# Seven block products in place of eight for three pairs of FFN chunks

## What is computed

```python
def swiglu(h, w_in, w_out):
    a, b = jnp.split(h @ w_in, 2, axis=-1)
    return (jax.nn.silu(a) * b) @ w_out
...
x = x + 0.5 * swiglu(rms_norm(x, norm_g[l, 0]), ffn_w_in[l, 0], ffn_w_out[l, 0])
```

## Time and profile before

| | us |
|---|---|
| median of 3 runs | 1055.21 (1054.1 to 1055.28) |
| the profiled execution, its own time | 1053.35 |
| its span | 1051.4 |
| PE busy in it | 1040.1 |
| DVE busy | 598.2 |
| ACT busy | 525.5 |
| POOL busy | 73.4 |

### The profile page before, as it was taken

How to read it: one execution, slowest core, us unless ns; L and a number is a source line. 1 busy time by engine, 2 the same in 40 slices (tenths; PEclk the granted TensorE clock), 3 DMA queues, 4 the chain that set the end, 5 groups by cost and what they waited for, 6 DMA issues and landing times.

```text
span 1051.4 us, 14153 instructions
## 1 busy us (share of the span) xinstructions
PE 1040.1 (99%) x5156; PEld 865.4 (82%) x5156; DVE 598.2 (57%) x833; ACT 525.5 (50%) x692; POOL 73.4 (7%) x108
## 2 busy tenths in 40 slices
PE   9999999999999999999999999999999999999997
PEld 7888888888888888888888888888888888888886
DVE  5554454677576564455467765544566656445544
ACT  7434434657475554434456554344356655443443
POOL 0041000000013000000000291000000000000000
PEclk9999999999899999999999999999999999999999
DMA  7686757457401366555545665555446146655541
GB/s 243 239 214 208 218 187 249 145 175 225 136 2 41 120 202 198 191 168 199 183 150 188 221 204 193 184 198 190 170 160 200 42 140 201 199 183 177 199 160 41
DMA packets 128709, 182.45 MB, mean 174 GB/s; under 512 B 5960, under 2 KB 100272, under 8 KB 128544
## 3 DMA queue, kind: packets, MB, share of 16 engines
q1 hardware_dynamic: 127040, 176.18, 50.5%
q0 software_dynamic: 1456, 5.72, 2.4%
q10 hardware_dynamic: 176, 0.05, 0.0%
HBM read 180.34 MB, written 1.59 MB: 173 GB/s over the span
## 4 chain that ended last, share of the span: by engine, by line
PE 97%; DVE 2%; ACT 1%; issue 0%; POOL 0%; POOLq 0%; DVEq 0%; ACTq 0%
PE inb L403 16%; PE inb L405 16%; PE inb L404 16%; PE acc L403 13%; PE acc L405 13%; PE acc L404 13%; PE acc L613 2%; PE tb L512 2%; PE tb L625 2%; PE inb L640 2%; PE inb L637 1%; PE tb L592 1%; PE tb L397 1%; PE acc L397 0%; DVE tlo L1346 0%; PE inb L824 0%
## 5 line engine op out<-in xcount | busy, mean ns | idle before, releaser
L1329 DVE TENSOR_TENSOR wlo<-raw,whi 128x2048 fp32r<-128x2048 f32 x108 | 250.0, 2315 | 233.6 <-ACT whi L935 233.6
L935 ACT CAST whi<-raw 128x2048 fp32r<-128x2048 f32 x108 | 206.5, 1912 | 217.5 <-PE acc L405 117.8
L403 PE MATMUL inb<-whi,thi 128*128 128x512 f32 x720 | 281.7, 391 | 0.0
L405 PE MATMUL inb<-whi,tlo 128*128 128x512 f32 x720 | 280.5, 390 | 0.0
L404 PE MATMUL inb<-wlo,thi 128*128 128x512 f32 x720 | 280.2, 389 | 0.0
L405 PEld LDWEIGHTS inb<-whi,tlo 128*128 128x128 f32 x720 | 135.1, 188 | 28.4
L404 PEld LDWEIGHTS inb<-wlo,thi 128*128 128x128 f32 x720 | 135.2, 188 | 28.0
L403 PEld LDWEIGHTS inb<-whi,thi 128*128 128x128 f32 x720 | 135.2, 188 | 28.0
L1312 DVE TENSOR_TENSOR wlo<-raw,whi 128x2048 fp32r<-128x2048 f32 x55 | 129.1, 2352 | 43.8 <-ACT whi L922 43.5
L403 PE MATMUL acc<-whi,ghi 128*128 128x512 f32 x320 | 128.5, 402 | 0.0
L405 PE MATMUL acc<-whi,glo 128*128 128x512 f32 x320 | 125.1, 391 | 0.0
(11 more groups left out here) (231 smaller groups left out, 980.1 us busy)
## 6 DMA issues: line engine op xcount, KB each, us to landing
raw<-in_ffn_w_in SPq DMA_DIRECT2D x174, 512.0 KB, 4.7
raw<-in_ffn_w_out SPq DMA_DIRECT2D x88, 512.0 KB, 4.0
raw<-in_nsa_w_in SPq DMA_DIRECT2D x20, 512.0 KB, 4.1
raw<-in_fox_w_kvf SPq DMA_DIRECT2D x16, 512.0 KB, 4.3
raw<-in_nsa_cmp_w SPq DMA_DIRECT2D x8, 512.0 KB, 4.8
raw<-in_nsa_w_out SPq DMA_DIRECT2D x8, 512.0 KB, 4.5
raw<-in_fox_w_q SPq DMA_DIRECT2D x8, 512.0 KB, 4.5
raw<-in_fox_w_out SPq DMA_DIRECT2D x8, 512.0 KB, 4.6
```

The costliest lines, as they stand in the source:

```text
L403: pe.matmul(o, lh, rh, start=start, stop=False, skip_group_check=True)
L405: return pe.matmul(o, ll, rh, start=False, stop=stop, skip_group_check=True)
L935: act.copy(whi[u % RING][:, :], raw[u % RING][:, :]).then_inc(s_hi, 1)
L1329: dve.tensor_tensor(wlo[u % RING][:, :], raw[u % RING][:, :], whi[u % RING][:, :].bitcast(F32), ALU.subtract).then_inc(s_lo, 1)
```

## The change

In each FFN three pairs of chunks (2 and 3, 5 and 6, 8 and 9) are projected together. Seen as blocks, a pair is a product of tokens (2 tiles x 2 halves of the 1024 columns, A11 to A22) and weights (2 halves of 512 rows x 512 gate or 512 up columns, B11 to B22). Seven products M1 to M7 replace eight. M1, M2 and M3 take B11, B21 and B22 as loaded; M5, M7, M6 and M4 take the combinations T1 to T4, which DVE makes (`t1_weights` to `t4_weights`); the token sides are A11, A12, A22 and the sums S1 to S4, which POOL makes once per FFN from the tokens, joined again from `thi` and `tlo` and scaled by rstd (`token_sums`). PE turns rstd into a row for that (`rstd_rows`). The results are put together on ACT and DVE: M1 to `u3`, M5 to `c22`, then `c12`, `u3` and `c22`, and C21 (`u3` again).

An ordinary chunk stands between two pairs. The loops are written out for all five engines. Ordinary units use two `raw` buffers; the third holds T1 and then T4. B11 and B12 go to `nat`, B21 to `xn`, B22 to the first part of `work`, loaded by SP with two DMAs of 512 KB each. T3 and T2 overwrite B12 and B11. The hidden halves get a buffer of four column blocks (`fhi`, `flo`). In FFN 2 the tables of the forget gate wait until the token sums are split. The last chunk is an ordinary one.

In the lists below, `wlo<-nat` or `wlo<-work` is the lo part of a weight unit, `flo<-tb` that of a turned hidden tile, `blo` that of a token sum; `raw<-nat`, `nat<-work,nat` and `nat<-nat` are T1, T3 and T2, and `raw<-xn,nat` is T4.

The core of the diff:

```diff
+KINDS = "nnsnsnsn"
...
+def ffn_order():
+    order = []
+    for kind, j, rows in SEGMENTS:
+        if kind == "n":
+            order += [("a", j), ("b", j)] + [("o", r) for r in rows]
+        else:
+            order += [("M1", j), ("M5", j), ("o", rows[0]), ("M2", j), ("M6", j)]
+            order += [("o", r) for r in rows[1:]] + [("M3", j), ("M7", j), ("M4", j)]
+    return order + [("o", r) for r in LAST_ROWS]
...
+            def product(f, j, name, a, bank, start, stop):
+                u = U_FFN[f] + UNIT_OF[name, j]
+                a_hi, a_lo = token_block(a)
+                pe.wait_ge(s_lo, u + 1)
+                for k in range(4):
+                    col = slice(k * CW, (k + 1) * CW)
+                    mm = three(bank[:, :], a_hi[:, k], a_lo[:, k], whi[u % RING][:, col], wlo[u % RING][:, col],
+                               start and k == 0, stop and k == 3)
+                mm.then_inc(s_used, 1)
...
+            def pair_turn(f, j, t):
+                pe.wait_ge(s_g, 2 * (NSEG * f + STAGES[j]) + t + 1)
+                pe.wait_ge(s_glo, NTURNS * f + turns_before(j) + t)
+                for k in range(4):
+                    mm = pe.transpose(tb[0][:, k * P:(k + 1) * P], (c22 if t else c12)[:, k * P:(k + 1) * P],
+                                      ident[:, :])
+                mm.then_inc(s_gt, 1)
+            def ffn_chunk(f, j, rows):
+                b, i = U_FFN[f], STAGES[j]
+                kind, before, _ = SEGMENTS[i - 1]
+                pairs = len(PAIRS) * f + sum(p < j for p in PAIRS)
+                u = b + UNIT_OF["a", j]
+                pe.wait_ge(s_lo, u + 1)
+                if kind == "s":
+                    pe.wait_ge(s_u3, pairs)
+                rows4(u % RING, 0, 0, inb[0][:, :])
+                if kind == "s":
+                    pe.wait_ge(s_c21, pairs)
+                rows4(u % RING, 0, 1, inb[1][:, :]).then_inc(s_used, 1)
+                if kind == "s":
+                    pair_turn(f, before, 1)
+                if before == 0:
+                    hidden_turn(f, 0)
+                    rstd_rows("kv" if f == 2 else f"ffn{f}")
+                unit_in((u + 1) % RING, 1, inb, u + 2)
+                for r in rows:
+                    out_rows(f, r)
+                hidden_turn(f, j)
+            def ffn_pair(f, j, rows):
+                n = len(PAIRS) * f + PAIRS.index(j) + 1
+                product(f, j, "M1", "A11", inb[1], True, False)
+                if j == PAIRS[0]:
+                    pe.wait_ge(s_alo, 4 * f + 1)
+                product(f, j, "M5", "S1", tb[1], True, False)
+                out_rows(f, rows[0])
+                pe.wait_ge(s_m1, n)
+                product(f, j, "M2", "A12", inb[1], False, True)
+                if j == PAIRS[0]:
+                    pe.wait_ge(s_alo, 4 * f + 2)
+                product(f, j, "M6", "S2", inb[0], True, False)
+                for r in rows[1:]:
+                    out_rows(f, r)
+                if j == PAIRS[0]:
+                    pe.wait_ge(s_alo, 4 * f + 3)
+                pe.wait_ge(s_m5, n)
+                product(f, j, "M3", "S4", tb[1], False, True)
+                if j == PAIRS[0]:
+                    pe.wait_ge(s_alo, 4 * f + 4)
+                pe.wait_ge(s_u2, n)
+                product(f, j, "M7", "S3", inb[0], False, True)
+                pair_turn(f, j, 0)
+                pe.wait_ge(s_silu, 2 * (NSEG * f + STAGES[j]) + 1)
+                product(f, j, "M4", "A22", inb[1], True, True)
...
+            def ffn_pair(f, j, rows):
+                b, i = U_FFN[f], STAGES[j]
+                m = {name: b + UNIT_OF[name, j] for name in ("M1", "M5", "M2", "M6", "M3", "M7", "M4")}
+                act.wait_ge(s_used, m["M1"] + 1)
+                if j == PAIRS[0]:
+                    act.wait_ge(s_an, 2 * f + 2)
+                act.mul(u3, inb[1][:, :], rstd[:, 0:1]).then_inc(s_m1, 1)
+                hi(m["M1"] + 3)
+                act.wait_ge(s_used, m["M5"] + 1)
+                if j == PAIRS[0]:
+                    act.wait_ge(s_as, 4 * f + 3)
+                    act.wait_ge(s_alo, 4 * f + 1)
+                act.copy(c22, tb[1][:, :]).then_inc(s_m5, 1)
+                hi(m["M5"] + 3)
+                hi(m["M5"] + 4)
+                act.wait_ge(s_used, m["M2"] + 1)
+                act.wait_ge(s_g, 2 * (NSEG * f + i))
+                act.activation(sa_p, inb[1][:, :], ACT.Silu, scale=rstd[:, 0:1]).then_inc(s_silu, 1)
+                hi(m["M2"] + 3)
+                hi(m["M6"] + 3)
+                for r in rows[1:]:
+                    hi(m["M6"] + 4)
+                hi(m["M3"] + 3)
+                hi(m["M7"] + 3)
+                pair_hidden_hi(f, j, 0)
+                act.wait_ge(s_c21, len(PAIRS) * f + PAIRS.index(j) + 1)
+                act.wait_ge(s_g, 2 * (NSEG * f + i) + 1)
+                act.activation(sa_p, u3, ACT.Silu).then_inc(s_silu, 1)
+                hi(m["M4"] + 3)

...
+            def tokens_lo(f, name):
+                dve.wait_ge(s_ahi, 4 * f + SPLITS.index(name) + 1)
+                a_hi, a_lo = token_block(name)
+                dve.tensor_tensor(a_lo, whole_block(f, name), a_hi.bitcast(F32), ALU.subtract).then_inc(s_alo, 1)
+            def t1_weights(f, j):
+                n = len(PAIRS) * f + PAIRS.index(j) + 1
+                dve.wait_ge(s_b11, 32 * n)
+                dve.wait_ge(s_b12, 32 * n)
+                dve.tensor_tensor(raw[(U_FFN[f] + 2) % RING][:, :], b12, b11, ALU.subtract).then_inc(s_tw, 1)
...
+            def ffn_chunk(f, j, rows):
+                b, i = U_FFN[f], STAGES[j]
+                kind, before, _ = SEGMENTS[i - 1]
+                a = b + UNIT_OF["a", j]
+                pair = SEGMENTS[i + 1][1] if SEGMENTS[i + 1:i + 2] and SEGMENTS[i + 1][0] == "s" else None
+                if kind == "s":
+                    pair_hidden_lo(f, before, 1)
+                elif before == 0:
+                    chunk_hidden_lo(f, 0)
+                if pair:
+                    t1_weights(f, pair)
+                lo(a + 3)
+                dve.wait_ge(s_gt, NTURNS * f + turns_before(j))
                 for t in range(NT):
-                    hidden_tile(n + t, t, banks)
-
-            def hidden_lo(n):
-                dve.wait_ge(s_ghi, n)
-                dve.tensor_tensor(glo[:, :, :].rearrange("p k n -> p (k n)"), tb[0][:, :],
-                                  ghi[:, :, :].rearrange("p k n -> p (k n)").bitcast(F32),
-                                  ALU.subtract).then_inc(s_glo, 1)
-
-            def hidden_last_lo(n, t):
-                dve.wait_ge(s_ghi, n)
-                tok = slice(t * P, (t + 1) * P)
-                dve.tensor_tensor(glo_last[:, :, tok], tb[0][:, :].rearrange("p (k n) -> p k n", k=2)[:, :, tok],
-                                  ghi_last[:, :, tok].bitcast(F32), ALU.subtract).then_inc(s_glo, 1)
+                    hidden_tile(2 * (NSEG * f + i) + t, t)
+                if pair:
+                    t3_weights(f, pair)
+                lo(a + 4)
+                if pair:
+                    t2_weights(f, pair)
+                for r in rows:
+                    u = b + UNIT_OF["o", r]
+                    chunk_hidden_lo(f, j)
+                    if pair == PAIRS[0]:
+                        for name in SPLITS:
+                            tokens_lo(f, name)
+                    if u + 3 < b + FFN_UNITS:
+                        lo(u + 3)
+            def ffn_pair(f, j, rows):
+                b, i = U_FFN[f], STAGES[j]
+                n = len(PAIRS) * f + PAIRS.index(j) + 1
+                m = {name: b + UNIT_OF[name, j] for name in ("M1", "M5", "M2", "M6", "M3", "M7", "M4")}
+                lo(m["M1"] + 3)
+                t4_weights(f, j)
+                lo(m["M5"] + 3)
+                lo(m["M5"] + 4)
+                lo(m["M2"] + 3)
+                dve.wait_ge(s_used, m["M6"] + 1)
+                dve.wait_ge(s_m1, n)
+                dve.wait_ge(s_gt, NTURNS * f + turns_before(j))
+                dve.tensor_tensor(c12, inb[0][:, :], u3, ALU.add).then_inc(s_u2, 1)
+                lo(m["M6"] + 3)
+                for r in rows[1:]:
+                    lo(m["M6"] + 4)
+                dve.wait_ge(s_used, m["M3"] + 1)
+                dve.wait_ge(s_u2, n)
+                dve.tensor_tensor(c12, tb[1][:, :], c12, ALU.add).then_inc(s_c12, 1)
+                dve.wait_ge(s_c12, n)
+                dve.wait_ge(s_silu, 2 * (NSEG * f + i) + 1)
+                dve.tensor_tensor(c12, c12, sa_p, ALU.mult).then_inc(s_g, 1)
+                lo(m["M3"] + 3)
+                dve.wait_ge(s_used, m["M7"] + 1)
+                dve.tensor_tensor(u3, inb[0][:, :], u3, ALU.add).then_inc(s_u3, 1)
+                dve.wait_ge(s_u3, n)
+                dve.wait_ge(s_m5, n)
+                dve.tensor_tensor(c22, c22, u3, ALU.add).then_inc(s_c22, 1)
+                lo(m["M7"] + 3)
+                pair_hidden_lo(f, j, 0)
+                dve.wait_ge(s_used, m["M4"] + 1)
```

(31 more changed lines are left out.)

459 lines of the change are left out of this document (301 added, 158 removed).

## The result

The changed kernel takes **1121.36 us** (median of 4 runs, 1118.62 to 1122.82), the old one beside it 1054.84: 1.0628 times as long, 95% interval 1.0605 to 1.0652. The forecast was 1088 and its range ended at 1106. The direction was right, the size was half of what came.

The account below looks back on a forecast made before the run. PE was taken to bound the kernel (busy 99%), with DVE becoming 90% full; -32.7 + 1.6 + 12.8 + 9.4 + 28.8 + 4.5 + 8 = +32.4 us on 1055.21 gave 1088 us, range 1040 to 1106.

Parts of the forecast that it names:

- 144 matmuls fewer: On PE, twelve pairs each need 12 fewer matmuls of 0.227 us: -32.7 us, if PE never waits.
- first pair's entry, with POOL: PE waits for M5 and output row 1, DVE slowed by POOL: 7.2 us four times, +28.8; bounds 2.5 and 9.5 each.
- later pairs: Two per FFN: PE waits for C12, C21 and the next entry, 1.6 us each, eight pairs: +12.8 us.
- first pair's body, and the tables: First pair's waits, 2.35 us four times: +9.4; FFN 2's forget-gate tables on POOL delaying DVE's splits: +8 us.
- boundaries 1 to 3: POOL's joining of token halves delays DVE's split of half b, 1.5 us in FFN 1, 2 and 3: +4.5 us.
- rstd rows: Two small PE matmuls that turn rstd in each FFN, 0.4 us four times: +1.6 us.
- Two buffers in place of three for ordinary loads: each load is issued over 10 us before its split: Ordinary weight loads with fewer raw buffers: claimed to cost nothing.
- PE's pace: 0.227 us each: Pace read from the 24 matmuls of one 512-row half of a chunk, 5.44 us.
- at nothing: Effects priced at zero: loads, two raw buffers, ACT's copies, the last chunk made ordinary; T1's transfers expected in time.
- rival 3: PE's clock falls after idling at the four entries: 12.8 us more, 1101 us, or 1110 with strict exclusion; chance 0.15.
- Rival 1: POOL's work beside DVE costs nothing, DVE keeps its pace: +1.1 us, so 1056 us; chance 0.15.
- Rival 2: Kernel gains if split-queue waits between M6 and C21 leave under 7.8 us per FFN: 1034 us; chance 0.2.

Follow-up runs that it names:

- five edits and no token sums: Changed kernel with raw buffers re-dealt, entry and C21 reordered, FFN 2's tables later, hidden tiles lower in SBUF, POOL writing constants instead of sums: 1060.08 us, ratio 1.0058.
- for four: Changed kernel with raw buffers re-dealt, entry reordered, C21 made earlier and FFN 2's tables later, all together: 1080.68 us, ratio 1.0258.

## Why the prediction was right in its terms and wrong in its sum

It forecast +32.4 us and +66.5 came. The terms it named, against the waits in the profile (spans: 1116.9 - 1051.4 = +65.5):

| term | forecast | measured |
|---|---|---|
| 144 matmuls fewer | -32.7 | as counted |
| first pair's entry, with POOL | +28.8 | 29.1 before M5, 38.5 up to output row 1 |
| later pairs | +12.8 | 11.3, and 0.5 in FFN 2 |
| first pair's body, and the tables | +9.4, +8 | 5.8 in FFN 0, 1, 3; 10.5 in FFN 2 |
| boundaries 1 to 3 | +4.5 | 4.7, of which the old kernel has 0.7 |
| rstd rows | +1.6 | 1.5 (0.37 each) |
| ends of FFN 0 to 2 | none | 7.1 |
| PE slow by the clock inside the FFNs | none | about 11, of which 9.4 in M5 at the entries |
| pace of the output rows | none | 5.3 (1056 x 0.0050) |
| pace of the chunk products with `thi`, `tlo` | none | 1.8 (1104 x 0.0016) |
| turns of chunks 0 and 1 | none | 2.6 |

The first six rows sum to 32.4 forecast and, with the entries taken before M5 alone, to about 31 measured. The prediction's view of DVE as the new limit, its places and its sizes held: 0.40 us for C12 and 1.01 us for C21 in later pairs (forecast 0.4 and 1.1), 1.5 to 1.7 us at boundaries (1.5). The loss of 34 us beyond it has three parts that are shown, and a fourth that looks like one and is none.

**"Two buffers in place of three for ordinary loads: each load is issued over 10 us before its split"** failed. It holds inside an FFN. At its end the next phase's first unit takes the buffer of the last output rows. The prediction had looked at the loop and not at the seam. In FFN 1 the load was issued at 562.47, the cast that waited for it began at 567.55 and the split at 569.49, 7 us behind the issue and not over 10. The run with other buffers gives 9.8 us back.

**"PE's pace: 0.227 us each"** was carried over to all matmuls. That the hidden tiles moved was plain in the diff, and the old kernel's last chunk, whose hidden tiles already lay in `fhi` and `flo`, ran its output rows at 0.2324 to 0.2344; the prediction did not read these rows. 5.5 us by the run at the low place.

**The entry** (7.2 us, four times) came out a third larger. The sum had 5.7 us before M5 and 1.5 before output row 1; 7.3 stood before M5, and with M5 slow 9.3 to 10.0 up to output row 1, 38.5 us in place of 28.8, so 9.7 more. With the clock held at 1.00 by filler the second wait appears by itself, 1.7 us, and the entry is as long. Two sizes were wrong. Without POOL the entries cost 3.8 us each and not 2.5: the wait for M5 was 2.2 and not 1.0, and T1's load, one of the transfers put "at nothing", lets DVE idle for 1.85 us there and for 2.04 in the changed kernel (both FFN 1). With POOL 5.9 more came (38.5 - 15.1 over four), not 4.7. Its 0.9 us for each of six instructions was right in the sum (in FFN 1 T1 lost 1.9, the two splits and T2 1.1 each and T3 0.3, 5.4 together), but the 0.6 us of idle time that was to take a part of it did not. The Trainium skill ("SBUF — State Buffer", Who interferes with whom) has the two exclude each other for a whole instruction; the rows of 3.2 to 3.4 us agree, and the end of 9.5 us that the prediction worked out for that case is the one that came.

**The clock** (rival 3) fell at the four entries as the rival said, to 0.51. Its price of 12.8 us on top was wrong: the gaps are there, about 11 us of them, but filling the wait gave 1.7 us back, within the measurement's spread, since DVE's next split was late anyway. Of the 11 us 9.4 are inside the 38.5 of the entries and can't be added to them; a part at the FFNs' ends went with the buffers.

Added up: ends 9.8 and place 5.5 by what runs gave back, the entries' 9.7 by the trace, 25 of the 34 us (22.5 with the two runs taken by their ratios). The waits at the turns of chunks 0 and 1 (2.6) and the products' slower pace (1.8) stand in the trace and were not tried apart. Some 5 to 7 us are not attributed; about 1.7 of these are at the program's start.

Rival 1 (POOL costs nothing) falls with the run in which POOL only writes: 29.5 us. Rival 2 (faster, the decision at 7.8 us of waiting per FFN) named the right point: the FFNs wait 14 to 26 us each. With five edits and no token sums they wait 6.3 to 8.8 us, 7.8 in the mean, and the kernel is 0.6% above the old one: the point lies there or a little lower.

## What to carry to other kernels

In this kernel, trading TensorE's matmuls for VectorE's element work would have paid only with room for VectorE in every stretch as long as its queue, not on the average. In a like case, count what each replaced product costs the engine that feeds it (here 2.7 us saved per pair against 15.5 us of added splits and combinations). Putting part of that work on GpSimd beside it added rather than divided here, where VectorE's instructions and GpSimd's both had two inputs in SBUF (3.4 us in place of 2.3, and 3.2 in place of 1.3). When a buffer count or an allocation changes, look at the seams between phases and at the pace of the matmuls whose stationary tiles (here the hidden tiles `fhi` and `flo`, 128x128 for each matmul) moved, not only at the loop.

## What the runs showed that was not expected

- The place in SBUF of the tile that PE loads as a matmul's stationary side changed its pace. With `fhi` and `flo` at 205.0 and 209.1 KB of each partition the output rows' matmuls start 0.2334 us apart, at 123.0 and 127.1 KB 0.2272, with nothing else changed but the tiles from `bhi` to `work`, 8.2 KB higher. The tiles at 200.9 KB in the old kernel were slow too (0.2324 to 0.2344). Where between 131 and 200 KB it begins wasn't tried, nor why.
- Edits that remove waits at different places gave more together than the sum of each alone (40.7 against 28.6 us for four, 39.0 against 21.5 by the ratios).
- A fallen clock can cost nothing: with 26 matmuls whose result nobody reads it stayed at 1.00 in place of 0.51, and the time was the same within 0.3%.
- Chunk products with `thi` and `tlo` as the stationary side run 0.2278 to 0.2287 us apart in the versions of the changed kernel and 0.2270 in the old one, at the same address. The written-out loops aren't the cause; it stays open.
